# Moving the four ysplit units of the Mamba branch from the group-norm generator to one place behind the last projection of the branch before

## The reference

```python
h = rms_norm(x, norm_w[layer])
proj = einsum('bsd,de->bse', h, w_in[layer])
(a_xbc, a_z, a_dt, b_q, b_k, b_v, b_z, c_q, c_k, c_v, c_f, c_z, gates) = split(proj)
y_a = mamba2_branch(...)            # ends in grouped_rms_norm(y * silu(z), norm_w, 4 groups)
y_b = sliding_window_branch(...)    # 16 heads, window 128, sinks
y_c = forgetting_attention_branch(...)
branch = einsum('bsiw,iwd->bsid', stack([y_a, y_b, y_c]), w_proj[layer])
merged = sum(sigmoid(gates + gate_bias[layer]) * branch, over the branches)
x = x + einsum('bsd,de->bse', merged, w_out[layer])
```

## Time and profile before

| | |
|---|---|
| time, median of 3 runs | 2188.44 us (2186.82 to 2188.52) |
| the profiled execution's time | 2188.52 us |
| its span, first to last instruction | 2186.8 us |
| mean granted TensorE clock | 0.980 of full speed |
| TensorE busy | 2085.0 us, 95% of the span |
| VectorE, ScalarE, GpSimd busy | 56%, 51%, 44% |

### The profile page before, as it was taken

The page is one execution under the profiler, slowest core; times in us unless marked ns, Lnnn a source line. Parts: engine busy times, 40 slices in busy tenths (PEclk is TensorE's granted clock), DMA queues, the critical chain, the costliest instruction groups (busy, mean ns, idle before and its releaser), DMA issues.

```text
span 2186.8 us, 36805 instructions
## 1 busy us (share of the span) xinstructions
PE 2085.0 (95%) x14870; PEld 1856.7 (85%) x14870; DVE 1230.1 (56%) x2034; ACT 1112.0 (51%) x1892; POOL 959.3 (44%) x424
## 2 busy tenths in 40 slices
PE   6999999999999999999999999999999989999997
PEld 6998998998898999988666876778888777898997
DVE  5577757345677655473464435455544546766565
ACT  5575476544585475554475233433333346645553
POOL 4655654653546555642112332323333233465662
PEclk9999999999999999999999999999999989999998
DMA  6454544565654544563212434333333333354551
GB/s 238 150 189 170 185 149 147 183 221 186 225 177 157 182 155 154 195 227 110 97 68 77 163 127 164 116 125 125 116 135 107 131 109 109 124 183 140 189 184 58
DMA packets 93321, 330.65 MB, mean 151 GB/s; under 512 B 10080, under 2 KB 13408, under 8 KB 92896
## 3 DMA queue, kind: packets, MB, share of 16 engines
q1 hardware_dynamic: 93152, 328.30, 43.6%
HBM read 327.08 MB, written 1.18 MB: 150 GB/s over the span
## 4 chain that ended last, share of the span: by engine, by line
PE 76%; DVE 11%; ACT 7%; issue 2%; DMA 2%; POOL 2%; SPq 0%; DVEq 0%; ACTq 0%; POOLq 0%
PE ps L878 21%; PE ps L879 21%; PE ps L880 21%; ACT t_hi L1239 2%; PE ps L932 2%; DVE t_lo L1554 1%; DMA t_A<-cu_scratch 1%; PE ps L891 1%; PE ps L892 1%; PE ps L893 1%; POOL t_lo L2021 1%; PE ps L1150 1%; DVE t_SQA L1564 1%; PE ps L1006 1%; PE ps L1160 1%
## 5 line engine op out<-in xcount | busy, mean ns | idle before, releaser
L2021 POOL TENSOR_TENSOR t_lo<-t_raw,t_hi 128x1024 fp32r<-128x1024 f32 (+1 forms) x360 | 884.9, 2468 | 1059.7 <-ACT t_hi L1239 1035.9
L878 PE MATMUL ps<-t_RB,t_hi 128*128 128x256 f32 (+1 forms) x3712 | 1170.8, 315 | 17.3 <-DVE t_RB L1842 5.3
L879 PE MATMUL ps<-t_RB,t_hi 128*128 128x256 f32 (+1 forms) x3712 | 1149.4, 310 | 0.0
L880 PE MATMUL ps<-t_RB,t_lo 128*128 128x256 f32 (+1 forms) x3712 | 1148.7, 309 | 0.0
L878 PEld LDWEIGHTS ps<-t_RB,t_hi 128*128 128x128 f32 x3712 | 712.3, 192 | 90.5 <-issue 31.5
L880 PEld LDWEIGHTS ps<-t_RB,t_lo 128*128 128x128 f32 x3712 | 712.6, 192 | 35.7
L879 PEld LDWEIGHTS ps<-t_RB,t_hi 128*128 128x128 f32 x3712 | 712.9, 192 | 34.9 <-issue 1.9
L1239 ACT ACTIVATE t_hi<-t_raw 128x1024 fp32r<-128x1024 f32 (+1 forms) x506 | 524.7, 1042 | 421.6 <-PE ps L880 387.9
L1554 DVE TENSOR_TENSOR t_lo<-t_raw,t_hi 128x1024 fp32r<-128x1024 f32 x146 | 211.2, 1447 | 264.4 <-ACT t_hi L1239 264.3
L1980 DVE SCALAR_TENSOR_TENSOR t_A<-ps,t_V,t_A 128x510 f32<-128x510 f32 (+1 forms) x176 | 102.2, 612 | 153.8 <-ACT t_A L1514 152.2
L1514 ACT ACTIVATE t_A<-ps,t_V 128x512 f32<-128x512 f32 (+1 forms) x88 | 48.5, 576 | 126.8 <-PE ps L880 126.8
(11 more groups left out here) (295 smaller groups left out, 2154.5 us busy)
## 6 DMA issues: line engine op xcount, KB each, us to landing
t_raw<-in_W SPq DMA_DIRECT2D x586, 512.0 KB, 3.5
t_A<-cu_scratch SPq DMA_DIRECT2D x8, 512.0 KB, 6.3
t_B<-cu_scratch SPq DMA_DIRECT2D x8, 512.0 KB, 4.4
t_raw<-in_W SPq DMA_DIRECT2D x16, 256.0 KB, 2.6
t_A<-in_C SPq DMA_DIRECT2D x2, 1536.0 KB, 6.8
t_X<-in_X SPq DMA_DIRECT2D x2, 512.0 KB, 4.4
t_X<-in_X SPq DMA_DIRECT2D x1, 1024.0 KB, 9.6
out<-t_X SPq DMA_DIRECT2D x1, 1024.0 KB, 4.8
```

The source lines that it names most:

```text
L878: mm(o, hi[:, w], xh(k), start=k == 0 and j == 0, stop=False)
L879: mm(o, hi[:, w], xl(k), start=False, stop=False)
L880: i = mm(o, lo[:, w], xh(k), start=False, stop=k == nkt - 1 and m == u.x[1] - 1)
L2021: tt(t.lo[s][:, 0:w], t.raw[r][:, 0:w], t.hi[s][:, 0:w].bitcast(F), ALU.subtract).then_inc(*up("pool", ("split", u.i)))
```

## The change

The generator `gnorm` no longer adds `ysplit`. All four `ysplit` units of the Mamba branch are added in one place, in `layer1`, after the fox branch's last `proj` and the step of the side generators behind it (which adds `gn 2` and `gn 3`), and ahead of the Mamba branch's first `gate`.

```diff
@@ gnorm
             self.add("gn", l=l, c=c)
             self.add("gn", l=l, c=c + 1)
             yield
-            self.add("ysplit", l=l, c=c, x=(0,))
-            self.add("ysplit", l=l, c=c + 1, x=(0,))
@@ layer1
         self.zgate(l, 0, O_ZA, None)
         for _ in rest:
             pass
+        for c in range(4):
+            self.add("ysplit", l=l, c=c, x=(0,))
         for _ in self.gated_proj(l, 0, None, False):
             pass
```

## The result

The changed kernel takes 2204.49 us (median of 4 runs, 2203.31 to 2207.19) against 2188.48 us before (4 runs, 2186.82 to 2189.1), both on the same chip; the ratio is 1.0074 with a 95% interval of 1.0059 to 1.0087. It is slower by 16.0 us. Four more runs of the changed kernel, which are not in that median, took 2201.61 to 2204.57 us. The span of the profiled execution of the changed kernel is 2201.0 us, 14.2 us more than before.

The account below looks back on a forecast made before the run. TensorE, busy 95% of the span, was taken as the bound, so order matters only through its idle time. 2188.52 + 12.47 of waiting + 4.4 for the clock = 2205.4 us, left at 2205; range 2198 to 2211 us.

Parts of the forecast that it names:

- the clock's term: TensorE's clock halves around the long gap ahead of pv 2 in each layer: 2.2 us a gap, 4.4 us for two.
- the wait for half-chunk 90: Layer 0, PE ahead of pv 2: the lo part comes at 352.1, asked for at about 351.4, a 0.7 us wait.
- ACT's queue is held, and 9.22 and 9.08 us of its work move behind ysplit 3: ACT, layers 0 and 1: split 90, gate 0, split 91, exp 3 and layer 1's like come after the waiting ysplits.
- gn 3 ends earlier by 3.30 and 2.53 us: DVE, layers 0 and 1: new order and no hold by POOL let gn 3 end and ysplit 3 start that much earlier.
- The part that came from POOL's idleness: DVE no longer held by POOL: 2.18 us earlier in layer 0, 1.04 and 0.38 us in layer 1.
- pv 2 moves by 5.92 and 6.55 us: PE: pv 2 starts later by moved ACT work less gn 3's gain, in layers 0 and 1; sum +12.47 us.
- proj 0 waits 0.9 us for ysplit 0: Layer 0, PE: proj 0's first half begins 0.9 us later, for ysplit 0's lo part; only shortens pv 2's wait.
- Nothing is given back: Behind pv 2 all queues stand to each other as before, so the whole +12.47 us lateness remains.
- a clock that falls at other places: Sign of a wrong prediction, in the trace after: the clock falls at other places than before; no size given.

Follow-up runs that it names:

- Experiment 1: Against the kernel before: only gn 2 and gn 3 moved ahead of ysplit 0 and 1, ysplit 2 and 3 left behind exp 3; 2189.52 us, ratio 0.9988.
- experiment 2: Against the kernel before: only ysplit 2 and 3 moved, right behind gn 3 and ahead of split 90; DVE order kept; 2207.54 us, ratio 1.0074.
- experiment 5: Changed kernel with exp 3, probs 3, turn 3 and pv 3 one step later, exp 3 behind turn 2; 2190.09 us, ratio 1.0001 to the kernel before.
- experiment 9: Changed kernel plus one extra POOL subtraction per layer between scores 3 and gn 2, without a result; 2207.19 us, ratio 1.0089 to the kernel before.
- experiment 4: Changed kernel plus 52 overwritten TensorE matmuls in each layer ahead of pv 2's wait; 2200.66 us, ratio 1.0051 to the kernel before.
- experiment 3: Changed kernel with the change in layer 0 alone, layer 1 as before; 2194.7 us, ratio 1.0025 to the kernel before.
- experiment 6: Kernel of experiment 1 with exp 3, probs 3, turn 3 and pv 3 one step later; 2188.45 us, ratio 0.9993 to the kernel before.
- experiment 7: Kernel before the change with exp 3, probs 3, turn 3 and pv 3 one step later; 2186.21 us, ratio 0.9992 to the kernel before.

## Why the prediction was right

It said 2205 us, 2198 to 2211; measured were 2204.49 us. The steps held; the clock's term was oversized, and the wait for half-chunk 90 a little too short. Step by step:

- *ACT's queue is held, and 9.22 and 9.08 us of its work move behind ysplit 3.* Right. Experiment 1 takes this step away and the loss is gone, experiment 2 has it alone and the loss is there, experiment 5 takes 5 us of exp and a table load out of the moved work and the loss is gone too. pv 2 started 363.46 - 347.75 = 15.71 us and 851.57 - 836.69 = 14.88 us behind ysplit 3; 6.64 + 9.22 = 15.86 and 5.80 + 9.08 = 14.88 us had been worked out.
- *gn 3 ends earlier by 3.30 and 2.53 us.* 351.31 to 347.75, less the 0.18 us, is 3.38 us; in layer 1 831.97 to 836.69 with 7.33 us of lateness is 2.61 us. The part that came from POOL's idleness was an inference from two coincidences of ends; experiment 9 made the hold come back. Of the two rules of the Trainium skill, the wide one ("GPSIMD Engine Reference", 1. Specifications) fits the changed kernel as well: line 1691, with two SBUF inputs, went from 1.21 to 0.17 us as POOL fell idle, where the narrow one would leave it.
- *pv 2 moves by 5.92 and 6.55 us.* 5.69 and 6.47 us.
- *proj 0 waits 0.9 us for ysplit 0 and 0.7 us for half-chunk 90.* 0.90 and 1.00 us. The wait for half-chunk 90 was 0.3 us longer because its lo part took 2.95 us on POOL (349.41 to 352.36), not 2.4. DVE was at the lo parts of ysplit until 350.12 then; the prediction had let POOL hold DVE and left out that DVE may hold POOL. In experiment 9, too, such a lo part took 2.95 us (from 351.92) beside the same four DVE instructions (350.14 to 352.63). pv 2's wait took the 0.3 us up, as was said.
- *The clock costs 2.2 us a gap.* 1.82 and 1.78 us: half clock lasted 3.8 us behind the gap, not 5.0. The prediction had not looked at when the clock fell: in its row 1.8 us of the 6.8 us at the low level lay inside the gap, here 3.0 of 6.8 us. The mechanism stood, experiment 4 shows it apart from the waiting; only the size was off, by 0.8 us in all. How far is a matter of the execution: behind the like waits of experiments 2, 3 and 9 half clock lasted 3.6 to 5.9 us.
- *Nothing is given back.* Right up to 973 us, 15.59 us. The prediction also named a clock that falls at other places as a sign that it is wrong. The missing fall near 1142 us is such a place, but it comes and goes with the same code, so it says nothing of the mechanism.

The sum had 12.47 + 4.4 = 16.9 us, the traces up to pv 3 of layer 1 have 12.16 + 3.60 = 15.8 us, the whole spans 14.2 us, and the runs 16.0 us. That the predicted time lies within 0.5 us of the median is partly luck: the eight runs of the changed kernel spread over 5.6 us. The wrong side of my expectations was the gain: experiments 1, 5 and 6 were each expected to win 0.7 to 2.1 us more than their rows show, because I followed one chain and left out what becomes the last wait once it is shorter (proj 0's end, or POOL's backlog on DVE). The times of 1 and 6 lie 0.5 us above their ranges, beside a kernel before that took 2189.6 us on those chips.

## What to carry to other kernels

In a list of units that every engine walks in order, moving a unit up also moves the wait of its first instruction ahead of everything that stood between: count the work on each queue that it passes, find which product waits for that work, and subtract what the moved wait itself gains. A wait on an engine that is half idle can be all but free by itself (with 8.95 us on ScalarE the runs of experiment 5 showed no loss); it costs when the critical engine needs what is queued behind. Before taking time off a chain, look for the second-latest input of the instruction at its end.

## What the runs showed of the hardware beyond that

- VectorE and GpSimd held each other by the instruction, in both directions. Four rows of the trace before, GpSimd first, tell it:

```profile
357.99 2.38 POOL L2021 TENSOR_TENSOR t_lo<-t_raw,t_hi 128x1024 fp32r<-128x1024 f32 x1 [2.62 <-ACT t_hi L1239]
360.32 2.85 POOL L2021 TENSOR_TENSOR t_lo<-t_raw,t_hi 128x1024 fp32r<-128x1024 f32 x1
...
358.19 2.72 DVE L1704 TENSOR_TENSOR t_B<-t_B,t_ST 128x512 f32<-128x512 f32 x1
360.84 3.42 DVE L1705 TENSOR_TENSOR t_B<-t_B,t_ST 128x1024 f32<-128x1024 f32 x1
```

Line 1704, 0.69 us long at 337.81 with GpSimd idle, ended 0.54 us behind GpSimd's first subtraction, so it got in between the two; the second one took 2.85 in place of 2.40 us meanwhile, and line 1705 (1.22 us at 338.42, where it came first) ended 1.09 us behind the end of that. In experiment 5, 3.22 us for an instruction of 1.23 us, it was the last of three subtractions that held VectorE. Reciprocals on [128, 256] were not held: 1.73 to 1.75 us in all eight cases of the trace before, among them the one at 826.33 in the earlier trace rows, while POOL worked from 826.14 to 828.68.
- TensorE's clock stood at 1.2 GHz for 3.8 us behind waits of 7.86 and 6.99 us, and work that filled such waits to 1.61 and 0.77 us kept it at 2.4 GHz. With these 104 extra matmuls the kernel was no slower and likely faster, by 3.8 us by the medians of two groups of runs whose intervals overlap a little.
- Two sigmoid units that follow each other on ScalarE with only copies between them need one table load: gate 1 had none in experiments 5 to 7. The load is moved, not saved, since exp 3 now stands between gate 1 and a later gate: each of the kernels has 84 table loads. What is gained is that 1.28 us no longer stand ahead of turn 2.
